# First output projection in two passes, with the memory attention beside its first pass

## What is computed

```python
h = _rms(x, norm_mix[0])
a, g, mq = split(h @ w_in_a, [768, 1536])
c, st = causal_dwconv(a * sigmoid(g), state, conv_a_w, conv_a_b)   # width 31
c = silu(_layernorm(c, ln_a_g, ln_a_b))                            # 768 channels
m = mem_attend(_rms(mq), mem_k[0], mem_v[0])   # 4 heads of 64, 256 memory rows
x = x + concatenate([c, m]) @ w_out_a          # 1024 x 1024
x = x + (gelu(dwconv3(h W_g)) * (h W_v)) @ W_down,   h = _rms(x, norm_ffn[0])
```

## Time and profile before

| | us |
|---|---|
| median of 3 runs (1451.43 to 1452.55) | 1452.32 |
| the profiled execution's own time | 1450.41 |
| its span in the profile | 1448.7 |
| PE busy | 1378.8 (95%) |
| DVE busy | 861.9 (59%) |
| ACT busy | 516.2 (36%) |
| POOL busy | 188.7 (13%) |

### The profile page before, as it was taken

How to read it: one execution, slowest core, us unless ns; L and a number is a source line. 1 busy time by engine, 2 the same in 40 slices (tenths; PEclk the granted TensorE clock), 3 DMA queues, 4 the chain that set the end, 5 groups by cost and what they waited for, 6 DMA issues and landing times.

```text
span 1448.7 us, 28167 instructions
## 1 busy us (share of the span) xinstructions
PE 1378.8 (95%) x11024; PEld 1284.8 (89%) x11024; DVE 861.9 (59%) x1721; ACT 516.2 (36%) x856; POOL 188.7 (13%) x245
## 2 busy tenths in 40 slices
PE   5999988999999999999999898898999999999997
PEld 5777767999999999999888776778999999999997
DVE  5444567566635663567776677775766436644652
ACT  4422356344312221224543444443534212221232
POOL 3323412220000000002102322320200000000001
PEclk8999999999999999999999999999999999999999
DMA  8344452243333333322323433332432333333222
GB/s 242 101 108 106 109 170 63 81 139 87 87 88 89 88 87 89 89 77 85 86 83 88 124 103 114 108 101 64 117 88 87 87 88 88 87 88 88 84 76 68
DMA packets 227822, 141.51 MB, mean 98 GB/s; under 512 B 9275, under 2 KB 217872, under 8 KB 227671
## 3 DMA queue, kind: packets, MB, share of 16 engines
q1 hardware_dynamic: 219295, 117.96, 28.8%
q0 software_dynamic: 7840, 21.89, 5.1%
q10 hardware_dynamic: 584, 0.23, 0.1%
HBM read 126.19 MB, written 7.85 MB: 93 GB/s over the span
## 4 chain that ended last, share of the span: by engine, by line
PE 79%; DVE 11%; ACT 4%; issue 2%; SPq 2%; DMA 1%; ACTq 1%; DVEq 0%
PE acc L549 64%; PE acc L764 3%; PE psT L706 3%; SPq L452 2%; DVE softmax_stats L2136 1%; ACT exps L1528 1%; PE acc L561 1%; DVE w_lo L1667 1%; ACT w_hi L1207 1%; PE psX L561 1%; DVE xa_lo L1712 1%; DVE psX L2134 1%; PE psT L1017 1%; DVE root_row L1700 1%; DVE x_resid L2019 0%
## 5 line engine op out<-in xcount | busy, mean ns | idle before, releaser
L549 PE MATMUL acc<-xa_hi,w_hi 128*128 128x272 f32 x1760 | 372.8, 293 | 6.9 <-DVE w_lo L1667 6.9
L549 PE MATMUL acc<-xa_hi,w_lo 128*128 128x272 f32 x1760 | 365.1, 289 | 0.0
L549 PE MATMUL acc<-xa_lo,w_hi 128*128 128x272 f32 x1760 | 363.9, 288 | 0.0
L1207 ACT ACTIVATE w_hi<-w_raw 128x1024 fp32r<-128x1024 f32 (+1 forms) x202 | 206.8, 1024 | 378.3 <-PE acc L549 346.4
L1667 DVE TENSOR_TENSOR w_lo<-w_raw,w_hi 128x1024 fp32r<-128x1024 f32 (+1 forms) x202 | 240.0, 1188 | 94.0 <-ACT w_hi L1207 92.5
L549 PEld LDWEIGHTS acc<-xa_hi,w_hi 128*128 128x128 f32 x1760 | 278.0, 189 | 17.9 <-issue 9.0
L549 PEld LDWEIGHTS acc<-xa_lo,w_hi 128*128 128x128 f32 x1760 | 277.5, 189 | 0.0
L549 PEld LDWEIGHTS acc<-xa_hi,w_lo 128*128 128x128 f32 x1760 | 275.9, 189 | 0.0
L549 PE MATMUL acc<-xb_hi,w_hi 128*128 128x272 f32 x896 | 194.0, 298 | 2.0 <-DVE xb_lo L2082 2.0
L549 PE MATMUL acc<-xb_hi,w_lo 128*128 128x272 f32 x896 | 185.3, 288 | 0.0
L549 PE MATMUL acc<-xb_lo,w_hi 128*128 128x272 f32 x896 | 184.7, 288 | 0.0
(11 more groups left out here) (338 smaller groups left out, 1723.7 us busy)
## 6 DMA issues: line engine op xcount, KB each, us to landing
w_raw<-in_w_up SPq DMA_DIRECT2D x88, 512.0 KB, 3.8
w_raw<-in_w_down SPq DMA_DIRECT2D x32, 512.0 KB, 3.9
w_raw<-in_w_in_a SPq DMA_DIRECT2D x14, 512.0 KB, 4.3
glu_shifted<-glu_rows SPq DMA_DIRECT2D x96, 67.5 KB, 2.0
w_raw<-in_w_down SPq DMA_DIRECT2D x16, 384.0 KB, 3.4
w_raw<-in_w_kv SPq DMA_DIRECT2D x12, 512.0 KB, 3.9
k_pages<-in_cache_k POOLq DMA_DIRECT2D x96, 64.0 KB, 2.3
v_pages<-in_cache_v SPq DMA_DIRECT2D x96, 64.0 KB, 2.1
```

Source lines behind the costliest of these rows:

```text
L549: last = nc.tensor.matmul(acc[slot][:, c, 0:n], w, x[:, k, c * n:(c + 1) * n], start=(k == 0 and q == 0), stop=(k == kb - 1 and q == 2))
L1207: nc.scalar.activation(whi[:, slot % 2, 0:n], wraw[:, slot, 0:n], ACT.Copy).then_inc(w_hi_ready, 1)
```

## The change

- The output projection of layer A becomes 16 steps: 8 of the 6 blocks of layer-normed channels (`ln_hi`, `ln_lo`, new tiles), then 8 of the 2 blocks of memory mix. Later steps are renumbered; the 8 second steps load, split and add to the residual like the others.
- The layer norm moves beside the memory projections: three chunks are centred on DVE and three on POOL, squares and sum stand between the splits, root, scaling, SiLU and parts at their end.
- The memory attention of layer A stands beside steps 15 to 29 by a table `aslots` like layer B's; `early(s, k)` is block k of step s, the other numbers count blocks of the first pass, 6 to a step. The cached scores take layer B's form (8 narrow matmuls for 4 samples at a time).
- In step 14 the last convolution chunk goes from behind block 0 to behind block 4, and the `tile_hook` of step 13 from behind block 1 to behind block 3.
- Roots of the memory queries, of the first keys and of the layer norm are taken by logarithm and exponential with a correction step on DVE (`inverted=True`), as layer B's are.
- The second layer's key squares and values turned, the keys turned for output and the convolution tail go into the last down-projection group of layer A's feed-forward part, with their copies on ACT and their stores on SP. The tail's turning goes from 12 transposes to 6.
- POOL loads the cached keys in two halves, the values behind the turning of each key tile, and has no stores of keys or tail.

```diff
...
-S_OUT = (S_MEM + 8, S_MEM + 8 + 8 + 68 + 20)
-S_FFN = (S_OUT[0] + 8, S_OUT[1] + 16)
+S_OUT = (S_MEM + 8, S_MEM + 8 + 16 + 68 + 20)
+S_FFN = (S_OUT[0] + 16, S_OUT[1] + 16)
 S_B = S_FFN[0] + 68
...
+def early(s, k):
+    return 8 * (s - S_OUT[0]) + k
+aslots = {
+    "S": (early(18, 3), early(20, 6), 7, 12, 17, 22, 27, 32),
+    "T": (early(19, 7), 1, 11, 16, 21, 26, 31, 36),
+    "O": (early(20, 4), 3, 13, 18, 23, 28, 33, 38),
+    "KM": (early(15, 2), early(15, 6), early(16, 6), early(17, 2), 9, 13, 18, 23),
+    "GM": (early(17, 6), 25),
+    "XT": (33,), "XV": (35,), "XO": (40,),
+}
+A_MIX = 43
+aturns = [(what, n) for _, what, n in sorted((g, what, n) for what in ("T", "KM", "XT", "XO")
...
         wo = a["w_out_a"][0] if l == 0 else a["w_out_b"][0]
         for m in range(KD):
-            if l == 0:
-                load(S_OUT[l] + m, block_cols(wo, m))
-                continue
-            load(S_OUT[l] + m, block_cols(wo, m, 0, HALF), kb=HALF)
-            if m in (1, 3, 5):
+            first = HALF if l else CC
+            load(S_OUT[l] + m, block_cols(wo, m, 0, first), kb=first)
+            if l and m in (1, 3, 5):
                 value_pages(3 + m // 2)
-        for m in range(KD if l else 0):
-            load(S_OUT[l] + KD + m, block_cols(wo, m, HALF, HALF), kb=HALF)
+        for m in range(KD):
+            load(S_OUT[l] + KD + m, block_cols(wo, m, first, KD - first), kb=KD - first)
         for g, (g0, n) in enumerate(GROUPS):
...
+            sp.wait_ge(mv_c, 2)
+            sp.dma_start(a["p_mem_v"][1][0].rearrange("(m p) h d -> p m (h d)", p=P), memv[:, 1, :, :]
+                         ).then_inc(st_mk, 16)
+            sp.wait_ge(ct_c, 2)
+            sp.dma_start(a["p_conv_a"][0][0], ctail[0:TAPS - 1, :]).then_inc(st_cs, 16)
+            sp.dma_start(a["s_conv_a"][0][:, TAPS - 1 - DS:, :], ctail[TAPS - 1:NTAIL, :]).then_inc(st_cs, 16)
+            sp.wait_ge(mk_c, 2)
+            for x in range(2):
+                sp.dma_start(a["p_mem_k"][x][0].rearrange("(m p) h d -> p m (h d)", p=P), mkn[:, x, :, :]
+                             ).then_inc(st_mk, 16)
             for c in range(MC):
...
     def conv_tail():
+        pe.wait_ge(ft_c, 1)
+        pe.wait_ge(ct_u, 2)
+        for j in range(CC):
+            last = nc.tensor.transpose(psT[0:NTAIL, j // 4, (j % 4) * P:(j % 4 + 1) * P], ctcol[:, j, :], ident)
         last.then_inc(ct_T, 1)
...
-        if k == 3 and s - 1 in tiles and s < S_MEM:
+        if k == 3 and s - 1 in tiles and s <= S_MEM:
             tile_hook(s - 1)
-        if conv_chunk(s) is not None and k == 0:
+        if conv_chunk(s) is not None and k == (4 if s == S_MEM else 0):
...
+        if (s, k) == (S_MEM + 2, 1):
             pe.wait_ge(conv_total, CC - 1)
             for c in range(2):
                 last = nc.tensor.matmul(psX[:, c, 0:HT], ones[:, :], csum[:, c * HT:(c + 1) * HT],
                                         start=True, stop=True)
             last.then_inc(ln_mean, 1)
+        if (s, k) == (S_MEM + 2, 3):
+            pe.wait_ge(aturn_taken, 2)
+            memory_key_squares(0)
+        if (s, k) == (S_MEM + 4, 1):
+            pe.wait_ge(taps_summed, CC)
+            memory_values_turned(0)
+        if (s, k) == (S_MEM + 6, 1):
+            pe.wait_ge(ma_exp, 1)
+            model_square_sum("ln", psX, CC)
+        if s > S_MEM:
+            beside_a(early(s, k))
...
+    def a_scores(m):
+        c, tb = divmod(m, QB)
+        if m == 0:
+            pe.wait_ge(qk_done, 4)
+            pe.wait_ge(as_c, 1)
+        else:
+            pe.wait_ge(ma_exp, m)
+        if m == 1:
+            pe.wait_ge(turned, RT["ln"] + 1)
+        if m == 6:
+            pe.wait_ge(as_c, 2)
...
+    def a_turn(m):
+        pe.wait_ge(ma_p, m + 1)
+        aturn_free("T", m)
+        for x in range(4):
+            last = nc.tensor.transpose(psT[:, 0, x * P:(x + 1) * P], et[:, m % 2, x * P:(x + 1) * P], ident)
+        last.then_inc(aturn_full, 1)
...
+    def a_weighted(m):
+        c = m // QB
+        pe.wait_ge(aturn_taken, aturn_at("T", m) + 1)
+        if m:
+            pe.wait_ge(ma_o, m)
+        else:
+            pe.wait_ge(mv_c, 1)
+        if m == 7:
+            pe.wait_ge(as_c, 3)
...
+    def a_turn_memory(b_):
+        if b_ == 0:
+            pe.wait_ge(mc_k0[0], 16 * DB // 2)
+            pe.wait_ge(taps_summed, CC - 1)
+        if b_ == 4:
+            pe.wait_ge(mc_k0[1], 16 * DB // 2)
+        if b_ == 2:
+            pe.wait_ge(mem_var, 1)
+        aturn_free("KM", b_)
...
+    def a_memory_weighted():
+        pe.wait_ge(aturn_taken, aturn_at("XT", 0) + 1)
+        pe.wait_ge(mc_v0, 16 * DB)
+        pe.wait_ge(ma_o, 7)
...
+    def beside_a(g):
+        for m in adue("O", g):
+            a_weighted(m)
+        for m in adue("T", g):
+            a_turn(m)
+        for b_ in adue("KM", g):
+            a_turn_memory(b_)
+        for _ in adue("XT", g):
+            a_memory_turn()
+        for _ in adue("XV", g):
+            a_memory_weighted()
+        for _ in adue("XO", g):
+            a_memory_turn_back()
+        for b2 in adue("GM", g):
+            a_memory_scores(b2)
+        for m in adue("S", g):
+            a_scores(m)
...
-    def out_section():
-        out_parts((0, 1), range(KD))
-        for m in range(2, KD):
-            out_parts((m,), range(KD))
+    for m in range(KD):
+        mm_step(S_OUT[0] + m, m % 2, ln_hi, ln_lo, kb=CC, hooks=lambda k, m=m: beside_a(CC * m + k),
+                ready=(lambda k: pe.wait_ge(cm_lo, k + 1)) if m == 0 else None)
+    for m in range(KD):
+        mm_step(S_OUT[0] + KD + m, m % 2, xb_hi[:, CC:KD, :], xb_lo[:, CC:KD, :], kb=MC,
+                ready=(lambda k: pe.wait_ge(cm_lo, CC + k + 1)) if m == 0 else None)
     def ffn(l, norm):
         def beside_down(m, k):
             if (m, k) == (1, 1):
                 ffn_tail(l)
+            if l == 0:
+                if (m, k) == (0, 3):
+                    memory_key_squares(1)
+                if (m, k) == (0, 5):
+                    memory_values_turned(1)
+                if (m, k) == (2, 4):
+                    conv_tail()
+                if (m, k) == (3, 2):
+                    memory_keys_out(0)
+                if (m, k) == (3, 4):
+                    memory_keys_out(1)
             if k == 3 and m:
                 after_chunk(l, m - 1)
...
+    split_hi(16)
+    a_turned_memory(0)
+    a_turned_memory(1)
+    split_hi(17)
+    act.wait_ge(acc_free, 16)
+    square(qf[:, 0, 0:2 * MEM], 2 * MEM)
+    act.wait_ge(ln_mean, 1)
+    nc.scalar.activation(csum[:, :].rearrange("p (c n) -> p c n", c=2), psX[:, :, 0:HT], ACT.Copy,
+                         scale=1.0 / CA).then_inc(ln_m, 1)
+    root(2 * MEM, inverted=True)
+    a_turned_memory(2)
+    split_hi(18)
+    ln_square(0)
+    a_turned_memory(3)
+    ln_square(1)
+    split_hi(19)
+    ln_square(2)
+    memory_values(0)
+    ln_square(3)
+    a_exponents(0)
+    split_hi(20)
+    ln_square(4)
+    ln_square(5)
+    split_hi(21)
+    a_turned_probs(0)
+    root(T, inverted=True)
+    a_exponents(1)
+    split_hi(22)
...
+    swish(1)
+    ln_high(0)
+    split_hi(23)
+    for j in range(2, CC):
+        swish(j)
+        ln_high(j - 1)
+    ln_high(CC - 1)
+    act.preload_act_table_set("natural_log_exp_and_others")
+    for m in range(KD):
+        for x in range(CC):
+            a_react(CC * m + x)
+        split_hi(S_OUT[0] + m + 2)
...
+            if l == 0:
+                square(qf[:, 0, 0:2 * MEM], 2 * MEM)
+                nc.scalar.activation(ctcol[:, :, 0:TAPS - 1], utl[:, :, :], ACT.Copy).then_inc(ct_u, 1)
+                nc.scalar.activation(ctcol[:, :, TAPS - 1:].rearrange("p c (b t) -> p c b t", t=DS),
+                                     usm[:, :, :].rearrange("p c (b t) -> p c b t", t=SEXT)[:, :, :, TAPS - 1:], ACT.Copy
+                                     ).then_inc(ct_u, 1)
...
+                if l == 0 and m == 1:
+                    root(2 * MEM)
+                    memory_values(1)
+                if l == 0 and m == 2:
+                    act.wait_ge(ct_T, 1)
+                    nc.scalar.activation(ctail[:, 0:512], psT[0:NTAIL, 0, :], ACT.Copy).then_inc(ct_c, 1)
+                    nc.scalar.activation(ctail[:, 512:CA], psT[0:NTAIL, 1, 0:CA - 512], ACT.Copy).then_inc(ct_c, 1)
+                if l == 0 and m == 3:
+                    memory_keys_out(0)
+                    memory_keys_out(1)
...
+    conv_take(CC - 1)
+    memory_take(14)
+    split_lo(16)
+    a_spread_queries()
+    memory_take(15)
+    split_lo(17)
+    memory_key_var(0)
+    ln_center(0)
+    memory_take(16)
+    ln_center(1)
+    split_lo(18)
+    memory_key_scale(0)
+    ln_center(2)
+    a_memory_first()
+    memory_take(17)
+    split_lo(19)
+    a_maxes(0)
+    memory_take(18)
+    split_lo(20)
+    a_normed(0)
+    memory_take(19)
+    split_lo(21)
+    dve.wait_ge(sq_used, SQ["ln"] + CC)
+    root_in(psX[:, :, 0:HT], T, 1.0 / CA, LN_EPS)
+    a_taken(0)
```

(55 more changed lines are left out.)

683 lines of the change are left out of this document (294 added, 389 removed).

## The result

The changed kernel takes 1459.38 us (median of 5 runs, 1458.40 to 1460.46) against 1452.32 for the kernel before (5 runs, 1451.43 to 1453.72): ratio 1.0049 with a 95% interval of 1.0038 to 1.0060. The forecast was 1454.7 in a range of 1446 to 1462: it lay on the right side, with two thirds of the difference missing (2.4 forecast, 7.1 measured).

A forecast was written before the change was run, and what follows sets the result against it. PE was taken as the bound after 301.67 except layer B's paged attention; small work bound the 47 us memory stretch. Terms -33.7 + 6.5 + 18.6 + 7.8 + 0.3 + 2.9 = +2.4 gave a median of 1454.7, range 1446 to 1462.

The forecast's parts named there:

- the square of step 13: Step 14: PE waits behind block 3 for step 13's square, from 161.7; wait 4.3 us.
- the values of step 18: Step 18: values turned behind block 1, their last tile taken late on DVE; PE waits 1.3 us.
- the first turning: Memory attention: PE waits 0.8 us for the division on DVE, queued behind `split_lo(20)`.
- the turned item in step 22: Step 22: behind block 3 PE waits for ACT's copy of turned item 1, behind a table load, done at 219.3.
- Part 2: Step 22 of the output projection: 11.0 us instead of 4.5, so +6.5 (5 to 9).
- Part 3: Steps 23 to 29: work beside 42 blocks of 31.8 us adds 18.6 (16 to 24); pass ends at 272.6.
- the rival of DVE's static order: First pass, slower: DVE's queue order makes PE wait at six turnings, 1.2 each, giving 1462; chance 0.20.
- Part 4: Second pass of the output projection: chain-bound, residuals 3.35 apart, 23.4 us; feed-forward part starts at 296.0 against 296.83.
- Part 5: Tails put into layer A's last down group, where PE has no gap, cost in full: +2.9 us.
- part 1: Up to the output projection's first block: ready at 211.2 against 244.94, -33.7 us; bounds 207.6 and 216.
- The faster one: Rival: waits up to the first block and in step 22 close up, -4.2 and up to -3.5, giving 1447; chance 0.25.
- The clock rival: Rival: feed-forward part starts at halved clock after the partly idle second pass, +1.7 or twice that, 1456.4 to 1458; chance 0.13.

The follow-up runs named there:

- two experiments that break the chain: Changed kernel with layer A's second-pass low part one step behind on DVE: 1455.46 us; or with the high part ahead of the square on ACT: 1451.93 us.

## Why the prediction was right in range and short by two thirds

**Right.** Where each wait would stand: the square of step 13, the values of step 18, the first turning, the turned item in step 22. Part 2: from the first block to the end of step 22 some 10.4, forecast 11.0, the table load worth 1.2. Part 3: 49.55 against 50.4, no wait at a turning, so the rival of DVE's static order was false. Part 4: 23.1 against 23.4, residuals 3.34 apart, so the lower count of blocks gives nothing, and two experiments that break the chain show that the chain was the bound. Part 5: 3.16 against 2.9; that it costs because PE has no gap there was shown by moving three of the tails (-1.5). The 0.66 for six transposes stands in none of the rows that the prediction names; the chain of the kernel before has it at 173.30.

**The step that was mis-sized is part 1**, -33.7 in the prediction and -28.8 measured. The first block of the output projection was ready at 217.05; less the 0.95 that the start came late, 216.1 instead of 211.2, at the edge of my bound. All of it lies ahead of the layer norm's sum: from there to the first block it is 12.2, forecast 12.1. The terms of these 4.9:

- 0.9: I had the table load of 1.28 ahead of step 14's high part in the text, and used it for the square, but began the walk of PE at 160.25 all the same. What stands behind that high part on DVE (low part, tap blocks, chunk, transposition) frees the accumulator that PE needs.
- 1.8: a wait of 4 us is not only 4 us. The hook took 1.3, the chunk 8.26 instead of 7.08, and the blocks around them more, at a granted clock of 0.77 in 166 to 171. I priced the clock in part 2 and for a rival, and not here.
- 1.7: the wait at the first turning is 2.46 instead of 0.8. Two of DVE's instructions ahead of it are held by POOL's totals, 1.27 instead of 0.17 and 1.50 instead of 0.70. I had bounded "DVE loses half a microsecond to POOL" and not taken it. This share is read from the trace; no run took POOL's totals away from there.
- 0.5 is left, small restarts that I didn't follow further.

That 216.1 falls just on my upper bound is luck: the bound named only POOL, and POOL explains at most 1.7 of the 4.9. It is luck too that 1459.4 lies above 1455.2, on the side that the chances gave mostly to the two slower rivals: neither of them came true in the first profile.

Parts 2, 3 and 4 gave back 1.75 of it (each a little cheaper than priced), so the feed-forward part started 3.1 later than forecast. With 0.3 more in part 5 and 2.3 of clock that the first profile caught at the start and in layer B, the profile's +8.0 is there: 2.4 + 3.1 + 0.3 + 2.3 = 8.1.

**The rivals.** The faster one failed by its own counter-argument: the waits come from the order of the queues and stayed. The clock rival came true in two of eight profiles, at 1.5 for the 1.7 given. The rival of DVE's order was false.

**Left open.** The medians differ by 7.1 and 7.4, the change's own stages by 5.8, or 5.2 against the second profile of the kernel before. The low clock at the first turning and at the feed-forward start in some runs adds to it; whether the longer stage in layer B (338.2 to 339.9 in five of ten profiles after, none of two before) is more frequent with the change, these few profiles can't say.

## What to carry to other kernels

A wait of PE costs its length and often the clock of what follows (1.8 us behind the wait of 4), and the next wait can take what the first one gave. So judge such edits together: ahead of the layer norm three of them gave 1.2, 0.3 and 1.4 alone and 4.2 together. When a pass is bound by a chain over several engines, look at the order inside the chain before the work in it: the instruction that others wait for goes first, here the high part ahead of the square. And before work is put on POOL, look at what DVE does at that time: in these traces its instructions that read two SBUF tensors, and its SBUF scalings, stand still until POOL's operation on tensors is over. The profile shows them as busy all the while, so the sign is not a pause but an end just behind the end of POOL's instruction.

## What was not expected of the hardware

- A DVE scaling of 128x2 took 1.27 us and one of 128x16 took 1.08, against 0.17 and 0.18, beside a POOL instruction of 1.3 to 1.4; they ended with it.
- A pass in which PE works 1.5 us of 3.35 kept the granted clock at 1.00 throughout (277.00 to 300.10). Behind such a pass the next matmuls ran at 1.00 in six of eight profiles, and near half clock in two.
- The same four fp32 matmuls of 272 columns took 1.08 us at full clock and 1.32, 1.92 or 2.18 behind a wait. Behind the same wait of 3.96 in step 14 they took 1.18 to 2.18 from profile to profile.
- A DVE instruction held by POOL ends a fixed time behind it, whatever the length of the hold: 0.28 us for 256 columns, 0.58 for 544, 1.08 for 1024, where the whole instruction alone is shown as 0.42, 0.78 and 1.23.
